# Second scan's low-rank gate product: rounded and low parts stacked along the contraction, one pass in place of float32

## The reference, cut to what matters

```python
def gla_prep(p, w_a2, b_a, with_q):
    a_lr = p[..., OFF_GLA_A:PROJ_WIDTH]              # (1, T, 2 * 16)
    la_f = log_sigmoid(a_lr[..., :16] @ w_a2[0] + b_a[0]) / 16.0
    la_b = log_sigmoid(a_lr[..., 16:] @ w_a2[1] + b_a[1]) / 16.0
```

## Time and profile before

| | |
|---|---|
| time, median of 3 runs | 1364.94 us (1364.13 to 1365.88) |
| the profiled execution, its own time | 1364.38 us |
| span of its trace, first to last instruction | 1362.7 us |
| PE busy | 1278.2 us (94% of the span) |
| DVE busy | 953.1 us (70%) |
| ACT busy | 773.2 us (57%) |
| TensorE clock granted, mean | 0.978 |
| the low-rank product, PE instructions | 16 of 592 ns and 8 of 378 ns |

### The profile page before, as it was taken

One profiled execution on the slowest core, in us unless ns is written; L12 is line 12 of the kernel. 1 busy time (PEld: TensorE's weight loads), 2 busy tenths in 40 slices (PEclk: granted clock), 3 DMA queues, 4 the chain that ended last, 5 costly groups with the idle time before them and its releaser, 6 DMA issues.

```text
span 1362.7 us, 19538 instructions
## 1 busy us (share of the span) xinstructions
PE 1278.2 (94%) x7427; PEld 1119.3 (82%) x7427; DVE 953.1 (70%) x1114; ACT 773.2 (57%) x918; POOL 119.2 (9%) x127
## 2 busy tenths in 40 slices
PE   5899999899999999989999399999999999999994
PEld 4888799898987999867888388888888888888883
DVE  5757420278655772476545878888888888888887
ACT  6643320375213644574334257777777777777785
POOL 1100000010000000013000020111111111111034
PEclk9999979999999999999999699999999999999997
DMA  9851151143445321304213879999999999999995
GB/s 369 271 120 34 62 158 44 39 137 121 155 186 185 124 81 76 140 1 170 81 75 140 322 267 367 388 406 397 397 397 395 397 394 397 391 402 392 400 318 207
DMA packets 78686, 320.45 MB, mean 235 GB/s; under 512 B 5544, under 2 KB 32200, under 8 KB 48856
## 3 DMA queue, kind: packets, MB, share of 16 engines
q1 hardware_dynamic: 71360, 291.18, 54.4%
q0 software_dynamic: 7264, 28.40, 8.3%
HBM read 292.20 MB, written 35.75 MB: 241 GB/s over the span
## 4 chain that ended last, share of the span: by engine, by line
PE 80%; DVE 10%; ACT 5%; DMA 3%; issue 2%; SPq 0%; POOLq 0%; DVEq 0%; ACTq 0%
PE psum L2538 36%; PE psum L2192 7%; PE psum L2474 6%; PE psum L2250 5%; PE psum L2251 5%; PE psum L2252 5%; PE psum L2278 1%; DMA ada_raw<-w_ada_units 1%; PE psum L2286 1%; PE psum L2287 1%; PE psum L2266 1%; PE psum L2093 1%; PE psum L2561 1%; ACT g_ps L1124 1%; PE psum L2555 1%
## 5 line engine op out<-in xcount | busy, mean ns | idle before, releaser
L1955 DVE TENSOR_TENSOR e_lo<-e_raw,e_hi 128x2048 fp32r<-128x2048 f32 x192 | 432.8, 2287 | 43.1 <-ACT e_hi L1274 43.0
L1274 ACT ACTIVATE e_hi<-e_raw 128x2048 fp32r<-128x2048 f32 x192 | 365.9, 1916 | 83.3 <-PE psum L2538 82.1
L2538 PE MATMUL psum<-e_hi,xt_hi 128*128 128x512 f32 x496 | 153.3, 390 | 0.1
L2538 PE MATMUL psum<-e_lo,xt_hi 128*128 128x512 f32 x496 | 152.9, 389 | 0.0
L2538 PE MATMUL psum<-e_hi,xt_lo 128*128 128x512 f32 x496 | 152.8, 389 | 0.0
L2250 PE MATMUL psum<-w_hi,h_hi 128*128 128x256 f32 x512 | 147.1, 287 | 0.5 <-issue 0.5
L2251 PE MATMUL psum<-w_hi,h_lo 128*128 128x256 f32 x512 | 145.8, 285 | 0.0
L2252 PE MATMUL psum<-w_lo,h_hi 128*128 128x256 f32 x512 | 145.8, 285 | 0.0
L2538 PEld LDWEIGHTS psum<-e_hi,xt_lo 128*128 128x128 f32 x496 | 93.1, 188 | 19.6
L2538 PEld LDWEIGHTS psum<-e_lo,xt_hi 128*128 128x128 f32 x496 | 93.1, 188 | 19.5
L2538 PEld LDWEIGHTS psum<-e_hi,xt_hi 128*128 128x128 f32 x496 | 92.8, 188 | 19.8 <-DVE xt_lo L1959 0.5
(11 more groups left out here) (414 smaller groups left out, 2330.3 us busy)
## 6 DMA issues: line engine op xcount, KB each, us to landing
e_raw<-w_e_units SPq DMA_DIRECT2D x192, 1024.0 KB, 7.6
ada_x<-w_ada_units SPq DMA_DIRECT2D x16, 1024.0 KB, 4.9
raw<-w_in_units SPq DMA_DIRECT2D x14, 1024.0 KB, 6.8
bc<-rows_dram SPq DMA_DIRECT2D x18, 512.0 KB, 3.8
ada_raw<-w_ada_units SPq DMA_DIRECT2D x8, 1024.0 KB, 21.8
xs<-x SPq DMA_DIRECT2D x4, 1024.0 KB, 12.5
acc_dram<-zero_r SPq DMA_DIRECT2D x1, 4096.0 KB, 19.6
wo_raw<-w_out SPq DMA_DIRECT2D x4, 1024.0 KB, 5.9
```

Of the source, the lines that this page charges most:

```text
L1274: act.activation(e_hi[u % EH][:], e_raw[u][:], ACT.Copy).then_inc(e_hi_ok, 1)
L1955: dve.tensor_tensor(e_lo[u][:], e_raw[u][:], e_hi[u % EH][:], ALU.subtract).then_inc(e_lo_ok, 1)
L2538: m = pe.matmul(o[:, BANK * b:BANK * (b + 1)], x[:, k, :], w[:, D * j + BANK * b:D * j + BANK * (b + 1)], start=a, stop=z)
```

## The change

The float32 matmuls are replaced by float32r matmuls over 96 rows, of which three groups of 32 carry the three products of the split: for each direction d a tile `zx[d]` holds the rounded rows in its own group (32 d), the low rows in the other of the first two groups, and the rounded rows again in rows 64 to 95. The weight tile `zw` holds rounded weights in rows 0 to 63 and low weights in rows 64 to 95. So hi x hi + lo x hi + hi x lo comes out of one matmul. ACT makes the rounded parts (6 instructions in two groups, one before and one behind the sigmoids of o1), DVE the low parts (3 instructions between columns 11 and 12), and TensorE waits for both before part 0. Two semaphores that already exist are used on. The host's constant array repeats the weights in three row groups; its size is the same.

```diff
+        zx = [at(f"zx{d}", AT_OUT + (36 + 5 * d) * KB, [P, ALL], F32R) for d in range(2)]
+        zw = at("zw", AT_OUT + 46 * KB, [P, 2 * GK_W], F32R)
+        zw_hi = at("zw_hi", AT_OUT + 48 * KB, [P, 2 * GK_W], F32R)
...
+        z_hi_ok, Z_HI = row_act, 4
+        z_lo_ok, Z_LO = row_dve, 1
...
             split_hi(17)
+            for d in range(2):
+                q = slice(32 * d, 32 * (d + 1))
+                act.activation(zx[d][q, :], gate_rows[q, :], ACT.Copy)
+            act.activation(zw_hi[64:96, :], col("w_gla2")[64:96, :], ACT.Copy).then_inc(z_hi_ok, 1)
             o_gates(1)
+            for d in range(2):
+                q = slice(32 * d, 32 * (d + 1))
+                act.activation(zx[d][64:96, :], gate_rows[q, :], ACT.Copy)
+            act.activation(zw[0:64, :], col("w_gla2")[0:64, :], ACT.Copy).then_inc(z_hi_ok, 1)
             split_hi(18)
...
-            ada_columns(10, 11, 12)
+            ada_columns(10, 11)
+            dve.wait_ge(z_hi_ok, Z_HI + 1)
+            for d in range(2):
+                q = slice(32 * d, 32 * (d + 1))
+                dve.tensor_tensor(zx[d][32 * (1 - d):32 * (2 - d), :], gate_rows[q, :], zx[d][q, :], ALU.subtract)
+            dve.tensor_tensor(zw[64:96, :], col("w_gla2")[64:96, :], zw_hi[64:96, :], ALU.subtract).then_inc(z_lo_ok, 1)
+            ada_columns(12)
             split_lo(18)
...
-                w = lambda dp: col("w_gla2")[:, P * dp:P * (dp + 1)]
+                if i == 0:
+                    pe.wait_ge(z_hi_ok, Z_HI + 2)
+                    pe.wait_ge(z_lo_ok, Z_LO + 1)
+                w = lambda dp: zw[0:96, P * dp:P * (dp + 1)]
                 if i < 8:
                     q = CTX + BANK * (i % 2)
-                    pe.matmul(z_ps(i), w(i // 2), gate_rows[:, q:q + BANK], start=True, stop=True).then_inc(z_mm, 1)
+                    pe.matmul(z_ps(i), w(i // 2), zx[i // 4][0:96, q:q + BANK], start=True, stop=True).then_inc(z_mm, 1)
                 else:
                     for j in range(2):
-                        x = pe.matmul(z_ps(i)[:, CTX * j:CTX * (j + 1)], w(2 * (i - 8) + j), gate_rows[:, 0:CTX], start=True, stop=True)
+                        x = pe.matmul(z_ps(i)[:, CTX * j:CTX * (j + 1)], w(2 * (i - 8) + j), zx[i - 8][0:96, 0:CTX], start=True, stop=True)
...
     for d in range(2):
-        w2[32 * d + NH:32 * d + NH + RANK, GK_W * d:GK_W * (d + 1)] = a["w_gla_a2"][0, d]
+        for q in range(3):
+            w2[32 * q + NH:32 * q + NH + RANK, GK_W * d:GK_W * (d + 1)] = a["w_gla_a2"][0, d]
```

## The result

| | before | after |
|---|---|---|
| median of 4 runs each | 1364.54 us (1363.11 to 1365.88) | 1354.99 us (1353.22 to 1357.15) |
| ratio, 95% interval | | 0.9931 (0.9912 to 0.995) |
| span of the profiled execution | 1362.7 us | 1351.5 us |
| mean granted clock | 0.978 | 0.978 |

The two traces differ by 11.2 us. I cut that difference in two, at the last sigmoid of o1: up to there TensorE's stream is the same in both programs, and I call that part the front. The stage itself comes first.

What follows compares the result with a forecast made beforehand. TensorE's stream was taken to bound the low-rank product's stage; cheaper parts save 5.24 + 1.29 = 6.5 us, new instructions cost nothing, so 1364.94 - 6.5 = 1358.4 us, range 1357.3 to 1360.9.

Steps and rivals of the forecast that it cites:

- What bounds it: Low-rank product's stretch, 414 to 447 us: TensorE's stream sets the time, busy 31.89 of 33.00 us.
- Cost of a part: Low-rank product's ten matmul parts: 0.883 us each falls to 0.228 for 512 columns, 0.240 for 256; saving 6.5 us.
- Rival B: Low-rank product: 96 rows count as a change of row number, 0.2 us a part; 1360.4 us, chance 0.09.
- Rival C: Low-rank product: row change stops the stream at each part; gain gone from 0.65 us a part, 1369.4 at 1.1; chance 0.03.
- The new instructions: ACT's copies, 3.2 us a group, and DVE's subtractions, 3.6 us, fit into waits before TensorE needs them; cost nothing.
- the cover that the prediction named: DVE's waits before column 12 and the split of unit 18, 5.4 us in all, hide its new subtractions.
- What is late next: Behind the parts: evacuations and columns keep up, TensorE turns columns 14 to 17 at 440.0, everything later moves 6.5 us earlier.
- rival D: Behind the stage: column 19's weights come late and TensorE waits before gv0's columns, 4.3 us lost; 1362.7 us, chance 0.05.
- Rival E: Low-rank product: the 96-row matmuls still run in two passes, time stays at 1364.9 us; chance 0.04.
- The absolute times that were named as signs: Trace of the changed kernel: column 12 starts near 395.9 us, TensorE turns columns 14 to 17 near 440.0.
- the runs' own spread of 0.9 either way: Whole kernel: run-to-run spread put around the forecast 1358.4, giving 1357.5 to 1359.3 us, chance 0.79.

Runs made afterwards that it cites:

- the fillers: Changed kernel with two 512-column matmuls, result unused, put among the statistics matmuls, where 14 were meant: 1357.71 us, ratio 0.9966 to the kernel before.

## Why the prediction was right in the stage and wrong in the range

- **What bounds it: right.** TensorE's stream sets the time of the stage before and after; ACT's evacuation is still the only other piece of the chain there, and still costs 1.11 us of idle time.
- **Cost of a part: right.** Forecast 0.228 and 0.240, shown 0.23 and 0.24; parts 1.60 us apart forecast, 1.61 shown. Forecast saving 6.5, shown in the stage 6.33 in the first pair of traces and 63.36 - 57.04 = 6.32 in the second. The missing 0.2 is the small price of 96 rows against the 128 from which I took the cost: over 128 rows the stage saves 6.53. Most of it is in the neighbours: six matmuls between parts take 1.38 where I took 1.367, over ten parts 0.13.
- **Rival B did not happen, but its price was set too low.** 96 rows don't count as a change: 0.02 us a part against 128 rows. A real change, to 64 rows, costs 1.98 - 1.61 = 0.37 us a part, not the 0.2 that I read from the float32 rows of the scan; it would have eaten 60.81 - 57.03 = 3.8 of the 6.3 us. The Trainium skill (TensorEngine Tiling (Array Packing), Key Properties) says that a change of tiling mode drains TensorE; the waits of the 64-row parts agree with it, 2.8 us before 8 parts and 2.0 behind them, and 96 rows, which its list (Available Configurations) doesn't have, show no drain.
- **Rival C: did not happen**, even at 64 rows: 0.37 is below its break-even of 0.65.
- **The new instructions: right.** ACT's first group fitted before its sigmoid with 0.28 us left; DVE's three took 2.97 + 0.68 = 3.65 us for 3.6. Counted in the times of the trace before (5.28 us later), column 12 starts at 396.0 for the 395.9 forecast, and the split at 401.7 for 401.7. The kernel with the new instructions alone shows 63.36 us for the stage, and doubling DVE's share 57.05: the cover that the prediction named holds.
- **What is late next: right, with one detail off.** The copy of unit 19 was bound by its load, as said, but waited 2.35 us for it and came 0.7 us earlier in the old times (423.32 + 5.28 = 428.60 for 429.31); no part waited for it. The turning came at 434.91 + 5.28 = 440.2 for the 440.0 forecast. Column 18 still waited 4.16 us for TensorE. Column 19 followed without a wait for its weights, and TensorE turned gv0's columns at 465.61 without idle time, so rival D did not happen. Rival E, two passes as before, is out by the one instruction that a part now is. The absolute times that were named as signs missed all the same: the columns turned at 434.91, not near 440.0, and column 12 started at 390.74, not near 395.9, since the sum took the front as fixed at the one trace that it had.
- **The failed step: "the runs' own spread of 0.9 either way".** That spread came from three runs, 1364.13 to 1365.88. The runs behind it cover 1358.73 to 1369.67. Both the base of the sum and the width of the range rested on it: the median 1364.94 from which I subtracted lies 1.9 us above the mean of 77 runs. With 1363.0 as base the same 6.5 gives 1356.5, and 18 runs gave 1356.1; from that base, a spread of 3 us either way would have held 1354.99. The 9.5 us of the first comparison are the 6.9 and what look like two lucky draws of four runs: 1364.54 - 1363.0 = 1.5 above the mean before, 1356.1 - 1355.0 = 1.1 below it after. The chip may have a part in this: the record doesn't say on which one the first comparison ran, and by chip the runs of the kernel before average 1362.8 to 1364.4. The prediction had the granted clock of its own trace at hand and read it only in the stage, where it was 1.00.

What is settled: the nine new instructions bring no gain (they alone gave 1.0011), and the kernel before has shown a front as short as one of the changed kernel's. What is open: why the clock falls where it does, though the length of the wait for DVE near 140 goes with an earlier fall (see the last section). In each trace one fall begins between 185 and 192, behind the start of the statistics or, without them, of the wait in their place, but the fillers were too few and the kernel without statistics was thin in another way, so no run shows that the one causes the other. And between the 6.3 us of the stage and the 6.9 of all runs, 0.6 us could still be an effect of the program in the front; the uncertainty of 1.0 doesn't separate it from none.

## What to carry to other kernels

A small float32 product inside a stream of float32r matmuls can be folded into one pass when its contraction leaves three groups of rows free: price it by the distance of starts, keep it off a row count that costs (here 64 rows cost 0.37 us a part and 96 next to nothing), and look for the splits' room on the engines that wait. Before forecasting a change of half a per cent, get the spread from more than three runs, and look at the granted clock over the whole span, not in the stage alone. Cut the difference of two traces at a landmark ahead of the change's effect: what has moved by then needs another explanation, and a second trace of each unchanged program shows how much it moves by itself.

## What the runs showed of the hardware that was not expected

- Matmuls over 96 rows between matmuls over 128 cost 0.02 us more a visit than 128 rows do; over 64 rows 0.37 us more than over 96, with the weight load idle 0.35 us on the way in and 0.25 on the way out.
- One unchanged program ran from 1358.73 to 1369.67 us over four chips, and from 1358.73 to 1367.71 on one of them. Its granted clock lay between 0.974 and 0.981, and the places where it fell between 60 and 460 us differ: 188 to 201, 259 to 263 and 338 to 341 us in one execution, and in another 141 to 144, 188 to 202, 260 to 263, 339 to 342 and 448 to 455.
- A fall can be made up again. Six of the fourteen traces (the changed kernel's first two among them) have the clock at 1.2 GHz for 3.4 to 6.9 us between 45 and 56; they reach the landmark of 83 us at 82.9 to 85.1, the eight others at 80.3 to 82.9. But the six then wait only 1.1 to 1.2 us for DVE near 140, the eight others 1.7 to 3.6.
- In five traces the clock fell within 1.4 us of the end of that wait, in which TensorE had stood idle for 2.29 to 3.59 us. In the first trace of the kernel before it had stood idle for 2.30 us and the clock stayed up.
- ACT's copy over 32 rows of 1280 elements takes 2.54 / 2 = 1.27 us, DVE's subtraction of that shape 2.97 / 2 = 1.48, the same as over 4 rows.
